# A first mixer whose indexer, gated attention and softmax steps are placed between half units of its projections

## The reference

```python
def _mixer_ab(x, w_in, w_gate, b_gate, g_norm, w_out, rel_table):
    y = x @ w_in
    qa, ka, va, ra, ga, qb, kb, vb, qi, ki, wi = _split(y, AB_SPLITS)
    g_log = jax.nn.log_sigmoid((ga @ w_gate + b_gate)) / GLA_GATE_TAU
    oa = _gla(qa, ka, va, g_log)                # gated attention, 4 heads of 64/128, chunks of 64
    oa = oa * rsqrt(mean(oa**2) + eps) * g_norm * silu(ra)
    ob = _dsa(qb, kb, vb, qi, ki, wi, rel_table)
    return concatenate([oa, ob]) @ w_out

def _dsa(...):
    score = einsum('bqh,bhqk->bqk', wi, relu(qi . ki))      # indexer, 8 heads of 64
    _, sel = top_k(where(causal, score, -inf), 64)          # choice of 64 keys per query
    logits = q . k * dh ** -0.5 + rel_bias                  # over the chosen keys alone
    return softmax(logits) @ v                              # 8 heads of 64
```

## Time and profile before

| | |
|---|---|
| device time, median of 3 runs | 1986.85 us (1984.53 to 1987.06) |
| time of the profiled execution | 1984.51 us |
| its span, first to last instruction | 1982.4 us |
| PE busy | 1868.7 us (94%) |
| DVE, ACT, POOL busy | 1374.0 (69%), 1110.4 (56%), 50.5 (3%) |
| mean granted clock of PE | 0.956 of full speed |
| chain that ended last | PE 87%, DVE 8%, issue 2%, ACT 2%, DMA 1% |
| loaded by SP's queue | 474.74 MB |

### The profile page before, as it was taken

One profiled execution on the slowest core, in us unless ns is written; L12 is line 12 of the kernel. 1 busy time (PEld: TensorE's weight loads), 2 busy tenths in 40 slices (PEclk: granted clock), 3 DMA queues, 4 the chain that ended last, 5 costly groups with the idle time before them and its releaser, 6 DMA issues.

```text
span 1982.4 us, 26182 instructions
## 1 busy us (share of the span) xinstructions
PE 1868.7 (94%) x10221; PEld 1589.4 (80%) x10221; DVE 1374.0 (69%) x1207; ACT 1110.4 (56%) x1031; POOL 50.5 (3%) x49
## 2 busy tenths in 40 slices
PE   6999899989979999999999999999999978779998
PEld 5897799968967878878888788787887858669997
DVE  3642544453468888888788888888988875955544
ACT  4532344434536767777776777776767743334343
POOL 0000100010020000000000000000000000010000
PEclk9997899988979999999999999999999988789999
DMA  9631455542357989999999899998999972314551
GB/s 283 223 128 56 159 189 190 184 137 83 128 171 273 372 312 366 343 328 369 333 345 370 308 367 344 334 372 307 365 342 333 366 264 83 120 64 164 186 190 43
DMA packets 252154, 490.43 MB, mean 247 GB/s; under 512 B 14178, under 2 KB 96651, under 8 KB 251716
## 3 DMA queue, kind: packets, MB, share of 16 engines
q1 hardware_dynamic: 248144, 474.74, 68.5%
q0 software_dynamic: 3184, 14.29, 2.2%
q10 hardware_dynamic: 772, 0.65, 0.1%
HBM read 488.56 MB, written 5.80 MB: 249 GB/s over the span
## 4 chain that ended last, share of the span: by engine, by line
PE 87%; DVE 8%; issue 2%; ACT 2%; DMA 1%; POOLq 0%; SPq 0%; DVEq 0%; POOL 0%; ACTq 0%
PE psum L525 26%; PE psum L527 25%; PE psum L528 25%; DVE ta L1940 2%; PE psum L966 2%; PE psum L1038 2%; PE psum L1012 1%; DVE wl L1501 1%; PE psum L586 1%; PE psum L671 1%; PE psum L613 1%; PE psum L645 1%; PE psum L618 1%; DVE u L1884 1%; PE psum L698 1%
## 5 line engine op out<-in xcount | busy, mean ns | idle before, releaser
L1501 DVE TENSOR_TENSOR wl<-ring,wh 128x2048 fp32r<-128x2048 f32 x446 | 1021.9, 2291 | 401.7 <-ACT wh L1131 401.2
L1131 ACT ACTIVATE wh<-ring 128x2048 fp32r<-128x2048 f32 x450 | 861.5, 1915 | 424.8 <-PE psum L525 354.7
L525 PE MATMUL psum<-wh,xTh 128*128 128x512 f32 (+1 forms) x1168 | 448.0, 384 | 7.1 <-DVE wl L1501 3.0
L527 PE MATMUL psum<-wl,xTh 128*128 128x512 f32 (+1 forms) x1168 | 438.0, 375 | 0.0
L528 PE MATMUL psum<-wh,xTl 128*128 128x512 f32 (+1 forms) x1168 | 437.8, 375 | 0.0
L525 PE MATMUL psum<-xTh,wh 128*128 128x256 f32 x1088 | 314.7, 289 | 13.9 <-DVE wl L1501 11.3
L527 PE MATMUL psum<-xTl,wh 128*128 128x256 f32 x1088 | 312.2, 287 | 0.0
L528 PE MATMUL psum<-xTh,wl 128*128 128x256 f32 x1088 | 311.9, 287 | 0.0
L525 PEld LDWEIGHTS psum<-wh,xTh 128*128 128x128 f32 x1168 | 221.8, 190 | 49.2 <-issue 10.8
L528 PEld LDWEIGHTS psum<-wh,xTl 128*128 128x128 f32 x1168 | 221.2, 189 | 41.0
L527 PEld LDWEIGHTS psum<-wl,xTh 128*128 128x128 f32 x1168 | 221.7, 190 | 39.9 <-issue 1.9
(11 more groups left out here) (260 smaller groups left out, 1215.4 us busy)
## 6 DMA issues: line engine op xcount, KB each, us to landing
ring<-in_w_moe SPq DMA_DIRECT2D x336, 1024.0 KB, 5.2
ring<-in_w_dense SPq DMA_DIRECT2D x33, 1024.0 KB, 5.2
ring<-in_w_in_ab SPq DMA_DIRECT2D x14, 1024.0 KB, 11.3
ring<-in_w_in_cd SPq DMA_DIRECT2D x12, 1024.0 KB, 5.3
ring<-in_w_gate SPq DMA_DIRECT2D x11, 1024.0 KB, 5.3
ring<-in_w_up SPq DMA_DIRECT2D x11, 1024.0 KB, 5.3
ring<-in_w_down SPq DMA_DIRECT2D x11, 1024.0 KB, 4.9
ring<-in_w_in SPq DMA_DIRECT2D x10, 1024.0 KB, 6.0
```

The source lines that it names most:

```text
L525: last = pe.matmul(o, a[0], b_[0], start=first, stop=False)
L527: pe.matmul(o, a[0], b_[1], start=False, stop=False)
L1131: act.activation(upper_half[i], ring[:, u_, :], ACT.Copy).then_inc(hi_ready[s_], 1)
L1501: dve.tensor_tensor(lower_half[i], ring[:, u_, :], upper_half[i].bitcast(F32), ALU.subtract)\
```

## The change

Mixer AB takes the form of mixer CD. Numbered gaps lie in the middle of each unit (2w-4) and behind it (2w-3), for units 2 to 13, and in the three first units of the output projection (24 to 28). PE, ACT and DVE each get a function `ab_gap(i)`:

- indexer group s stands in gap s (0 to 7); the gated attention's products in gap 14, its outputs in gap 16, its exponentials on ACT in gaps 6, 8, 10 and 11, its operands on DVE in gap 12, its norm in gap 20;
- scores of the softmax groups in gaps 17 to 20 and 22 to 25, turns one or two gaps later, values one more; the order of the groups is now by quarter (two pairs of heads for the first half of the queries, the same two for the second half), in banks 0, 1 (scores), 2 (turns) and 3 (values);
- the output is turned in pieces of two blocks (`turn_out`) in gaps 21, 21, 26 and 28, into `uTh`/`uTl` and `xTh`/`xTl`, instead of all at once;
- the order of units is now: indexer queries, qa, ka, va, va, then the first halves of qb, kb, vb, then ra, ra, and the second halves of qb, kb, vb;
- `top_keys` is cut into pieces of one or two rounds, one in most gaps from 3 to 16;
- the key mask is written as a rounded (one-pass) tile `keymask` in the place of `score`, and added as a one-pass product with a rounded identity `ident_r`;
- the rows of relative bias are made right behind the transposes of x: `rel` has a 33rd row of ones and `onehot` a 33rd row of masks, so that one product makes each. `ident`, the two tables and `onehot` are loaded from ACT's queue at its start, `ident` no longer by SP; the other constants are 7 loads instead of 11. On POOL the load of `lnw` moves behind the spreading of the rows and the load of `bias`;
- the narrow products of the gate and the weights (24 columns) come ahead of those of the indexer's keys; `gko` lies in `pr` instead of `nv`.

Mixer CD changes in the counts of its waits alone.

```diff
+AB_INDEXED = [0, 1, 2, 3, 4, 5, 6, 7]
+AB_SCORES = [17, 18, 19, 20, 22, 23, 24, 25]
+AB_TURNED = [19, 20, 21, 22, 23, 24, 25, 26]
+AB_VALUES = [20, 21, 22, 23, 25, 26, 26, 27]
+AB_OUT_TURNED = [21, 21, 26, 28]
...
-            def group_scores(g, q, k, forget=False):
+            def group_scores(g, q, k, forget=False, masked=False):
...
+                    if masked:
+                        last = pe.matmul(o, ident_r[:, :], keymask[:, t, 0:n], start=False, stop=True)
...
             transposes(x, 0)
+            pe.wait_ge(rel_const, 48)
+            for i, w in enumerate((0, 0, 1)):
+                ps = step_bank()
+                pe.matmul(ps[0:8, 0:REL], rel[:, w, :], onehot[:, i, :], start=True, stop=True).then_inc(step_done, 1)
             proj_transposed()
             proj_transposed()
...
-            for i, w in enumerate((0, 0, 1)):
-                ps = step_bank()
-                pe.matmul(ps[0:8, 0:REL], rel[:, w, :], onehot[:, w, :], start=True, stop=False)
-                pe.matmul(ps[0:8, 0:REL], ones[0:1, 0:8], rowadd[:, i, :], start=False, stop=True).then_inc(step_done, 1)
...
+            def ab_gap(i):
+                for s in at(AB_INDEXED, i):
+                    index_scores(s)
+                if i == 14:
+                    gla_products()
+                if i == 16:
+                    gla_outputs()
+                for s in at(AB_SCORES, i):
+                    if s == 4:
+                        pe.wait_ge(o_low, 2)
+                    if s % 4 == 0 or s == 2:
+                        pe.wait_ge(mask_ready, 1 if s == 0 else 2)
+                    group_scores(s, tq, tk, masked=True)
+                for s in at(AB_TURNED, i):
+                    group_turn(s, bank[2], s)
+                for s in at(AB_VALUES, i):
+                    group_values(s, nv, bank[3], s // 4)
+                for j in at(AB_OUT_TURNED, i):
+                    if j < 2:
+                        pe.wait_ge(gla_done, 1)
+                    turn_out(j, bank[j % 2], max(j - 1, 0), (4, 4, 8, 8)[j])
+
+            for w in range(2, AB_UNITS):
+                middle = lambda: ab_gap(2 * w - 4)
+                if w in (2, 3, 6, 7, 11, 12):
+                    proj_transposed(middle)
+                else:
+                    proj_natural(middle)
...
+                if w == 3:
+                    gate_sums()
+                ab_gap(2 * w - 3)
             pe.wait_ge(step_evac, steps[0])
-            pe.wait_ge(mask_ready, 1)
-            attention(0, tq, tk, nv, values_projected_0, masked=True)
-            pe.wait_ge(a_done, 2)
-            transposes(u)
-            out_projection()
+            for j in range(4):
+                out_unit(j, j + 1, (lambda: ab_gap(24 + 2 * j)) if j < 3 else None)
+                if j < 3:
+                    ab_gap(25 + 2 * j)
...
+            for w in range(2, AB_UNITS):
...
+                ab_gap(2 * w - 4)
+                if w == 2:
+                    copy_step(tb[:, 0:2, :], scale=HD ** -0.5)
...
                 upper()
...
+                ab_gap(2 * w - 3)
...
+                for t, first, final in {3: [(0, 0, 2)], 5: [(0, 2, 3)], 7: [(0, 3, 5)], 8: [(0, 5, 7)], 9: [(0, 7, 8), (1, 0, 0)],
+                                        10: [(1, 0, 2)], 11: [(1, 2, 4)], 13: [(1, 4, 5)], 15: [(1, 5, 6)],
+                                        16: [(1, 6, 8)]}.get(i, ()):
+                    top_keys(t, first, final)
...
+            for w in range(2, AB_UNITS):
+                ab_gap(2 * w - 4)
+                ab_gap(2 * w - 3)
                 lower()
...
-            weights(0, (ln_g[0, 0:1, :], ln_b[0, 0:1, :]))
-
             for i in range(3):
-                pool.wait_ge(step_evac, 7 + i)
+                pool.wait_ge(step_evac, 1 + i)
                 pool.dma_start(rel_rows[i], relrow[:, i, :]).then_inc(rel_out, 16)
...
             bias_table(0)
+            weights(0, (ln_g[0, 0:1, :], ln_b[0, 0:1, :]))
```

More of the change, by code:

```diff
@@ L50 @@
 STEPS_CONV = 53
-CONSTS = 16 * 11
+CONSTS = 16 * 7
 NARROW = 168
@@ new lines, in gla_outputs @@
+            def gla_outputs():
+                pe.wait_ge(gla_Am, 4)
+                pe.wait_ge(step_evac, 14)
+                for h in range(4):
+                    v_ = slice(h * P, (h + 1) * P)
+                    first_of(pe.matmul(bank[4][:, v_], gA[:, h, 0:P], nw[:, 0, v_], start=True, stop=True))
+                    pe.matmul(bank[5][:, v_], gA[:, h, P:T], nw[:, 0, v_], start=True, stop=False)
+                    last = pe.matmul(bank[5][:, v_], gA[:, h, T:384], nw[:, 1, v_], start=False, stop=True)
+                last.then_inc(gla_o, 1)
@@ L1247, in ffn @@
                     upper(down_done[s], NCH_D)
+            act.dma_start(ident[:, :], c_ident).then_inc(ident_in, 16)
+            act.dma_start(rel[0:32, 0, :], rel_table).then_inc(rel_const, 16)
+            act.dma_start(rel[0:32, 1, :], rel_bias_2).then_inc(rel_const, 16)
+            act.dma_start(onehot[:, :, :], c_onehot).then_inc(rel_const, 16)
+            act.wait_ge(ident_in, 16)
+            act.activation(ident_r[:, :], ident[:, :], ACT.Copy)
             copy_transposed()
             upper()
+            for i in range(3):
+                act.activation(relrow[:, i, :], step_out()[0:8, 0:REL], ACT.Copy).then_inc(step_evac, 1)
             upper()
@@ L1323, in _, with ab_gap @@
-            copies(tk[:, 0:2, :], tk[:, 2:4, :])
-            attention(0, lambda: copies(nv[:, :, 0:256], nv[:, :, 256:512]))
-            copy_transposed()
-            upper()
-            upper()
+            def ab_gap(i):
+                for s in at(AB_INDEXED, i):
+                    index_relu(s)
+                for s in at(AB_TURNED, i):
+                    group_copy(s, bank[2])
+                if i == 6:
+                    gla_exps(0, (0, 1))
+                if i == 8:
+                    gla_exps(0, (2, 3))
+                if i == 10:
+                    gla_exps(1, (0, 1))
+                if i == 11:
+                    gla_exps(1, (2, 3))
+                if i == 16:
+                    act.wait_ge(gla_o, 1)
+                    for t in range(TT):
+                        act.activation(y[:, t, 0:512], bank[4 + t][:, :], ACT.Square).then_inc(gla_sq, 1)
+                for s in at(AB_SCORES, i):
+                    group_exps(s)
+                for j in at(AB_OUT_TURNED, i):
+                    out_upper(j, bank[j % 2], j + 1)
@@ L1328, in _ @@
+            for j in range(2):
+                ab_gap(24 + 2 * j)
+                upper()
+                ab_gap(25 + 2 * j)
+            ab_gap(28)
             upper()
@@ L1441, in _, with copies @@
                .then_inc(step_evac, 1)
+            def copies(*dsts):
+                for dst in dsts:
+                    copy_step(dst)
+                    upper()
             copy_step(ta[:, 0:2, :])
@@ L1687, in _, with index_sum @@
             log_sigmoid(gz[:, :, :], ga_[:, :, :], gnat[:, :, :], 1)
-            for i in range(8):
+            def index_sum(i):
                 t, hp, n = i // 4, i % 4, P * (i // 4 + 1)
@@ L1760, in two_units @@
+            for w in range(2, AB_UNITS):
+                ab_gap(2 * w - 4)
+                ab_gap(2 * w - 3)
                 lower()
+            for j in range(2):
+                ab_gap(24 + 2 * j)
+                ab_gap(25 + 2 * j)
                 lower()
-            two_units()
-            dve.wait_ge(rel_in[0], 16)
-            attention(0, relative(), 512, two_units)
-            lower_transposed()
-            two_units()
+            ab_gap(28)
             halves.skip()
```

350 lines of the change are left out of this document (180 added, 170 removed).

## The result

| | before | after |
|---|---|---|
| device time, median of 4 runs each | 1986.95 us (1984.53 to 1988.94) | 1959.09 us (1956.83 to 1963.81) |
| ratio after / before, 95% interval | | 0.9862 [0.9849, 0.9874] |
| time of the profiled execution | 1984.51 us | 1958.01 us |
| its span | 1982.4 us | 1955.9 us |
| PE busy | 1868.7 us | 1840.5 us |

What follows compares the result with a forecast made beforehand. PE was taken as the bound, busy 94% of the span and 87% of the chain. Eight terms summed to -30.2 us, from 1984.5 to 1954.3; with the median somewhat above, the forecast was 1955 us, range 1946 to 1968.

Steps and rivals of the forecast that it cites:

- term 8: Start: first unit lands earlier without lnw beside it, spreads move to about 20 us beside units 2 to 7; -2.0 us.
- Rows of relative bias: Ahead of the indexer: six products leave PE's path, three new ones fit into PE's wait for the first unit; -7.0 us.
- Softmax attention: Mixer AB's attention: 57.9 us stretch becomes 31.1 at full clock, with sixteen one-pass masks of 0.12 us; -26.8 us.
- Rival C: Attention masks: a one-pass mask costs what several passes take, 6.5 us, giving 1961; chance 0.05.
- changing of kinds: Gaps between half units: a half unit with steps on both sides takes 3.05 us against 2.9, over 22 gaps; +3.3 us.
- Two slow half units: New attention: two half units run at half speed, 4.53 for 3.05 us, as some in mixer CD; +3.0 us.
- Late halves: DVE's lower halves: unit 7 late by 1.2 us, gap 22's scores by 0.7, with a little more; +2.5 us.
- rival A: Start: the spreads delay the ring, unit 3 lands near 39 us, some 8.5 us lost, giving 1963; chance 0.15.
- All behind stays as long: Layer norm, dense part and everything behind start earlier but keep their length, the ring being full; no gain or loss.
- Rival B: Units 4 to 11: DVE becomes the bound, 1.5 us late at each of eight, 12 us, giving 1967; chance 0.15.
- Rival D: Most gaps: the clock falls, 14 more half units take 4.5 us, +21, giving 1976; chance 0.06.
- Rival E: Gaps 17 to 28: PE's scores wait for DVE's maximum, 4.8 us per missed gap; nine missed give 1998; chance 0.04.

Runs made afterwards that it cites:

- e6: The kernel before with only the new head (relative-bias rows behind the transposes of x, loads moved, spreads late); mixer AB otherwise unchanged; 1978.51 us.
- e3: e1 with the key mask as a full 32-bit, several-pass product again; 1949.85 us.
- e8: e1 with both heads' products before the masks, ACT's first gated exponentials in gaps 7 and 9, first turned-output pieces in banks 4 and 5; 1941.73 us.
- e9: e8 with the rounds of the choice of keys taken out of gaps 3, 5 and 7 and regrouped into gaps 8 to 16; 1940.38 us.
- e7: e1 with the choice of keys in two whole pieces, eight rounds each in gaps 8 and 15; 1949.48 us.
- e1: The changed kernel with one more wait on POOL, holding the bias-row spreads and loads behind them until unit 3's result is copied; 1946.49 us.
- e10: The changed kernel with sixteen extra, unread one-pass products of 256 columns behind the gated attention's outputs; 1966.65 us.
- e5: The kernel before with the one-pass key mask and rounded identity alone, nothing placed otherwise; 1980.66 us.

## Why the prediction was right, and where it was wrong

The main mechanism, steps between half units at full clock, held. The closeness of the total is luck: term 8 missed by 14.0 us, and 8.9 us that no term named came back behind the mixer.

1. **Rows of relative bias (-7.0): right here, not by itself.** In the changed kernel next to no cost shows ahead of the first unit: ACT's last copy of a row lets PE begin at 14.44, and DVE's lower half was done at 14.34. By itself (e6) the step gives 3.3: the cover it removes hid ACT's log-sigmoid. The prediction asked what covers the new products, not what the old ones had covered.
2. **Indexer (-1.5): a little better.** The groups took 0.42 and 0.63 us, 4.2 against 4.8.
3. **Softmax attention (-26.8): right in kind.** Full clock as assumed; the masks were 0.31 and 0.23 us at 256 columns and 0.16 to 0.26 at 128 instead of 0.12 each, some 2 us more in all. Rival C (the price of several passes) is out by e3: they cost 3.4 more.
4. and 5. **Idle time (-1.7), changing of kinds (+3.3): held.** The old idle time went, and term 7's took its place: PE is idle for 1.7 us between the start of unit 2 and the attention in both kernels. At full clock half units took 2.95 to 3.1.
6. **Two slow half units (+3.0): none in the attention.** Its window shows 1.00. The slow clock that stayed is that of the gated products and the start (0.92 from 50.72 to 126.60).
7. **Late halves (+2.5): right in size (1.7 at unit 7, 0.3 at gap 22), wrong in cause.** Not ACT's exponentials (e8) but rounds of the choice queued behind a sum that waits for PE's gap 7 (e9).
   Terms 1 to 7 together: -29.6 measured, -28.2 forecast.
8. **Start (-2.0): wrong, +12.0.** The gain came (first projection 2.7 us earlier), and rival A on top, given 0.15. The last output product, looked for near 176 us, ended at 189. The step that failed is "nearest is the gain": the case against A was that SP had issued units 2 and 3 before the spreads. It had; but issued is not served. Unit 3 had 1.7 us before the first spread was issued, then shared 22 us with 4.5 MB. The Trainium skill ("DMA: Bandwidth & Descriptors", Queues, rings and completion order) lets each DMA engine take turns between queues that have work, and the prediction wrote that by that rule A was to be expected if the margin did not hold; the trace agrees so far as unit 3 took 27.96 us for 10.6. A's price was also short, 8.5 against 14.8: it took the delay as half of 18 us and left out the slow clock behind the stop, 17.1 us from 38.5 on, through the gate's product and most of unit 2's first half.
9. **"All behind stays as long": wrong, -8.9.** It offset most of term 8's miss, and nothing in the prediction earned it.

Rival B (DVE the bound) is out: PE waited for one lower half, 1.7 us, and e7 shows the slack. Rival D: in no profile of the new attention did a half unit run slow. Rival E: no gap was missed; PE's list of waits has none for DVE's maximum.

Without the ring's wait (e1) the norm's transposes begin 34.7 us earlier than in the kernel before (177.89 for 212.61), for 30.2 forecast: -3.0 at the start, -31.7 for terms 1 to 7.

## What to carry to other kernels

A transfer that is moved to an earlier time must be set against every transfer then in flight, issued or not: moving 4.5 MB of spreads 30 us forward, with 2 MB of loads behind them, cost more than any other step, and one wait on the issuing queue gave 12.6 us back. Ask of removed work what it covered on other engines, and of a late buffer what stands ahead of it in the queue of the engine that makes it, waits included. And give a change's downstream time a band of its own: here the same code took 1761 to 1770 us, so a gain under some 9 us in such a kernel needs the windows of the changed stage, not the total alone.

## What was not expected of the hardware

- Sixteen products worth 2.0 us, put into a stretch that is otherwise unchanged, made the kernel 7.6 us slower by the medians (e10): PE's busy time in the untouched stretch behind rose by 5.3 us.
- Steps of attention placed between half units of a projection run at full clock, with one-pass masks as with full ones (e3), while the same steps in a row ran at half clock for much of their length with either (mean 0.68 in e5, 0.71 before).
- A one-pass product of 256 columns takes 0.12 us from start to start among its own kind, and 0.23 to 0.31 between 32-bit products of several passes.
- What stays open: which event in PE's past sets the moment at which the clock falls; the runs show only that it moves with a shift of 2 us, and that each of two kernels repeated its own downstream time in a second profile.
